# Spreading an expert's token weights over the partitions: two float32 passes from 32 rows, or one float32r matmul from 128 rows

## The chip, the cores and the metric

The kernel runs on one core of one Trainium2 chip. The metric is the device time of one execution in microseconds; the median of three runs is given, and one further execution was profiled.

## The reference, cut to what matters

The program is a chain of 18 stages on 256 tokens of 1024 features. Two of the stages (stage 1 and stage 4) are mixtures of experts; eight are feed-forward stages of a like shape. What an expert stage computes:

```python
g_w, g_idx = lax.top_k(softmax(xt @ w_group + b_group), 1)        # one of 4 groups
e_w, e_idx = lax.top_k(softmax(logits of that group), 2)          # two of its 8 experts
cw = einsum('tk,tke->te', g_w * e_w / sum(e_w), one_hot(expert))  # 256 tokens x 32 experts
hid = silu(einsum('td,edf->tef', xt, w_gate)) * einsum('td,edf->tef', xt, w_up)
y = einsum('tef,efd->td', hid * cw[:, :, None], w_down)
```

All 32 experts are computed for all tokens, and `cw` holds zeros for the experts that a token did not choose. A feed-forward stage is the same without `cw`, with 22 units of 128 hidden features.

## The kernel before

Activations lie feature by token: a tile of 128 partitions holds 128 features of 256 tokens. A product in float32 is made from three matmuls in float32r, a type in which TensorE takes one pass: weight and activation are each split into a high half (ScalarE copies to float32r) and a low half (VectorE or GpSimd subtracts the high half), and `mm3` (L591) adds high by high, high by low and low by high.

Weights stream through a ring of four slots (`ring`), one transfer of 1536 KB for one unit, issued in a fixed order by SyncE. From a slot a unit's three pieces (gate, up, down) are split into `wp`, which holds eight pieces; a piece's place is taken again once TensorE has used the old piece. In some of the units one more 1536 KB slot is read for work that belongs to later stages: ScalarE (`ada_act`) and VectorE (`ada_dve`) sum it into `ada_acc`, and one unit later TensorE (`ada_pe`) adds it up over the partitions with three float32 matmuls against `ones`. In an expert stage this starts in units 2, 4, ..., 30, and the three matmuls are issued in units 3, 5, ..., 31.

`glu_pe` sets the order on TensorE. For unit u it issues `products(u)` (48 float32r matmuls into one PSUM bank: gate in its left half, up in its right half), then what hooks and `ada_pe` there are, then `spread(u)`, then `down(u - 1)` (24 float32r matmuls that add into the stage's output in banks 0 to 3). `spread(u)` takes row u of `cwT`, a tile of 32 experts by 256 tokens, to all 128 partitions: the stationary operand is column u of the identity, broadcast over 128 columns, and both operands are float32 of 32 rows. The profile shows one float32 matmul call as two instructions.

The first two units have no `spread` and no `down` yet, for `cw` is not known. They come in unit 2 (`g.first` is 2), in the order `spread(0)`, `spread(1)`, `spread(2)`, `down(0)`, `down(1)`. Before them TensorE turns `cw` (L1598), and VectorE takes it out of PSUM and multiplies it with the token's scale into `cwT` (L1682).

`glu_dve` and `glu_act` hold the hidden part of a unit, which starts when `products(u)` is done: VectorE scales the gate (`rsb`), ScalarE takes Silu, VectorE multiplies with up, then with the spread weights, ScalarE makes the high half in `ex` and VectorE the low half. `down(u)` waits for the last of these. In each unit VectorE and ScalarE first split the next unit's pieces, then do the `ada` work where there is one, then the hidden part. In the last unit the pieces that are split first are those of the next stage. `spread(u)` waits for a free bank; in unit 2, `spread(1)` takes the bank of `products(0)` and `spread(2)` that of `products(1)`, each once VectorE has read the up half.

In the traces the matmuls carry the line of the helper `mm` (L271), so that they are told apart by their tiles: `pb<-hx,wp` is `products`, `pb<-ex,wp` is `down`, `pb<-ones,ada_acc` is `ada_pe`, and `pb<-sq,cst` is `spread`. `pb` is PSUM, `cwT` lies in `sq`, the identity in `cst`.

Of the kernel before, what the change touches and what calls it, by code (L numbers as in the profile page):

```python
# [11 lines left out]
FR = mybir.dt.float32r  # L12
I32 = mybir.dt.int32
ACT = mybir.ActivationFunctionType
AX = mybir.AxisListType

T = 256
# [307 lines left out]
def build_program(nc, stop=None):  # L325
# [6 lines left out]
    def sb(name, cols, dt=F32, rows=128):  # L332
        return ctx.enter_context(nc.sbuf_tensor(name, [rows, cols], dt))
# [34 lines left out]
    selw, selg = sb("selw", 128), sb("selg", 64)  # L368
    hr, bsum = sb("hr", 256, rows=48), sb("bsum", 256, rows=16)
    dl = sb("dl", 32)  # L370

    WK = 23 * 1024 - 64
    with nc.sbuf_tensor("wk", [128, WK], F32) as region:
# [45 lines left out]
    def row_spread(h, rows):  # L419
        a = ccol["ident"][0] + h  # L420
        return cst[0:rows, a:a + 1].to_broadcast([rows, 128])
# [25 lines left out]
    def bank(*key):  # L447
        return pb[where.get(key, 0)]
# [415 lines left out]
    def glu_pe(e, g, ready, hooks=(), cw=None):  # L864
        st = g.st
        bk.use([4, 5, 6, 7])

        def products(u):
            key = (st, "glu", u)
            ps = bk.take(e, key, (v_out, key))  # L870
            if u == 0:
                pair = g.pieces[u][0:2]
                for p in pair:
                    split_ready(e, p)
                for k in range(KD):
                    for sig, event in ready(k):
                        e.wait_ge(*sig[event])
                    for b, p in enumerate(pair):
                        ins = mm3(e, ps[:, b * T:(b + 1) * T], part((p.hi, p.lo), k * 128), in_hx(k), k == 0 == b,
                                  k == KD - 1)  # L880
                ins.then_inc(*product.up(("used", pair[0].at), ("used", pair[1].at), key))
                return
            for b, p in enumerate(g.pieces[u][0:2]):
                split_ready(e, p)
                for k in range(KD):
                    for sig, event in ready(k):
                        e.wait_ge(*sig[event])
                    ins = mm3(e, ps[:, b * T:(b + 1) * T], part((p.hi, p.lo), k * 128), in_hx(k), k == 0, k == KD - 1)
                ins.then_inc(*product.up(("used", p.at), *([key] if b else [])))

        def spread(u):
            key = (st, "cw", u)
            ps = bk.take(e, key, (v_out, key))
            e.wait_ge(*v_out[st, "cwT"])
            e.mm(ps[:, 0:T], row_spread(u, 32), cw, True, True).then_inc(*summed.up(key))

        def down(u):
            p = g.pieces[u][2]
            split_ready(e, p)
            e.wait_ge(*x_lo[st, "hid", u])  # L900
            for m in range(8):
                if u == 0 and m % 2 == 0:
                    y = bk.hold(e, m // 2, (st, "y", m // 2), (x_new, (st, m + 1)))
                y = pb[m // 2]
                ins = mm3(e, y[:, (m % 2) * T:(m % 2 + 1) * T], part((p.hi, p.lo), m * 128), (eh[u % 3], el[u % 3]),
                          u == 0 and m % 2 == 0, u == g.units - 1)
                if m % 2:
                    ins.then_inc(*product.up((st, "down", u, m), *([("used", p.at)] if m == 7 else [])))

        for u in range(g.units):  # L910
            products(u)
            if u < len(hooks):
                hooks[u]()
            if u in g.summed:
                ada_pe(e, g.summed[u])
            if u >= g.first:
                if cw is not None:
                    for n in range(0 if u == g.first else u, u + 1):
                        spread(n)
                for n in range(0, u) if u == g.first else [u - 1]:  # L920
                    down(n)
        down(g.units - 1)
        bk.use(range(8))
# [620 lines left out]
    def moe(st, l, slot0, after):  # L1544
# [32 lines left out]
        def pe(e):  # L1577
            def norm_and_logits():
                bk.hold(e, 0, (st, "var"), (v_step, (st, "var")))
                for k in range(KD):  # L1580
                    e.wait_ge(*g_step[st, "square", k])
                    ins = e.mm(bank(st, "var")[:, 0:T], ones[:, 0:128], Q3[:, k, :], k == 0, k == KD - 1)
                ins.then_inc(*summed.up((st, "var")))
                bk.hold(e, 1, (st, "lg"), (v_out, (st, "lg")))
                for k in range(KD):
                    ins = e.mm(bank(st, "lg")[0:36, 0:T], wr[:, k, :], H3[:, k, :], k == 0, k == KD - 1)
                ins.then_inc(*summed.up((st, "lg")))

            def logits_by_token():
                bk.hold(e, 2, (st, "lgt"), (v_out, (st, "lgt")))  # L1590
                e.wait_ge(*v_step[st, "lgT"])
                for b in range(2):
                    ins = e.tp(bank(st, "lgt")[:, b * 36:(b + 1) * 36], lgT[:, b * 128:(b + 1) * 128])
                ins.then_inc(*turned.up((st, "lgt")))

            def weights_by_expert():
                bk.hold(e, 3, (st, "cwt"), (v_out, (st, "cwT")))
                e.wait_ge(*v_step[st, "cw"])  # L1598
                for b in range(2):
                    ins = e.tp(bank(st, "cwt")[0:32, b * 128:(b + 1) * 128], cw[:, b, :])  # L1600
                ins.then_inc(*turned.up((st, "cwt")))

            glu_pe(e, G_, ready, (norm_and_logits, logits_by_token, weights_by_expert), cwT)

        def first_max(e, src, n, mx, eq, cum, oh, event):
            e.red(flat(mx), src, ALU.max).then_inc(*v_step.up())
# [48 lines left out]
        def dve(e):  # L1655
            for k in range(KD):
                e.ts(H3[:, k, :], X3[:, k, :], gain(k), None, ALU.mult).then_inc(*v_step.up((st, "h", k)))
                e.wait_ge(*v_step[st, "h", k])
                e.wait_ge(*x_hi[st, "h", k])
                e.tt(Hl[:, k, :], H3[:, k, :], Hh[:, k, :], ALU.subtract).then_inc(*x_lo.up((st, "h", k)))  # L1660

            def norm_and_logits():
                split_lo_v(e, G_.pieces[1])
                e.wait_ge(*summed[st, "var"])
                e.wait_ge(*v_step.last)
                e.ts(nv[:, :], bank(st, "var")[:, 0:T], 1.0 / D, 1e-6, ALU.mult, ALU.add).then_inc(*v_step.up((st, "var")))
                newton(e, rsb[:, :], nv[:, :], nm[:, :], nt[:, :], (st, "rs"))
                e.wait_ge(*v_step[st, "rs"])
                e.wait_ge(*summed[st, "lg"])
                e.tt(lgT, bank(st, "lg")[0:36, 0:T], rsb[0:36, :], ALU.mult).then_inc(*v_out.up((st, "lg")))  # L1670
                e.wait_ge(*v_out[st, "lg"])
                e.ts(lgT, lgT, pc(f"moe_b{l}", 0, 1, 36), None, ALU.add).then_inc(*v_step.up((st, "lgT")))

            def logits_by_token():
                e.wait_ge(*turned[st, "lgt"])
                e.copy(lg, bank(st, "lgt")[:, 0:72].rearrange("p (b n) -> p b n", b=2)).then_inc(*v_out.up((st, "lgt")))
                split_lo_v(e, G_.pieces[2])
                choose(e)

            def weights_by_expert():  # L1680
                e.wait_ge(*turned[st, "cwt"])
                e.tt(cwT, bank(st, "cwt")[0:32, 0:T], rsb[0:32, :], ALU.mult).then_inc(*v_out.up((st, "cwT")))  # L1682

            def finish(m, ps):
                e.tt(X3[:, m, :], X3[:, m, :], ps, ALU.add).then_inc(*x_new.up((st, m)))

            glu_dve(e, G_, finish, (norm_and_logits, logits_by_token, weights_by_expert), True)

        def act(e):
            for k in range(KD):  # L1690
                e.wait_ge(*x_new[st - 1, 7])
                e.act(Hh[:, k, :], X3[:, k, :], ACT.Copy, scale=gain(k)).then_inc(*x_hi.up((st, "h", k)))

            def norm_and_logits():
                split_hi(e, G_.pieces[1])

            def logits_by_token():
                split_hi(e, G_.pieces[2])
                for name, a in (("ge", ge), ("e2", e2)):
                    e.wait_ge(*v_step[st, name])  # L1700
                    e.act(a, a, ACT.Exp).then_inc(*a_step.up((st, name)))

            glu_act(e, G_, (norm_and_logits, logits_by_token, lambda: None), True)

        def pool(e):
            for k in range(KD):
# [1045 lines left out]
    def scalar_program(e):  # L2752
        e.wait_ge(s_in, 48)
        e.act(cact[:, :], pc("c", 0, 8), ACT.Silu).then_inc(*a_step.up("cact"))
        for s in stages:
            s.act(e)

# [64 lines left out]
```

## Time and profile before

| | |
|---|---|
| median of 3 runs | 4298.62 us (4298.27 to 4301.55) |
| the profiled execution: its time, its span | 4305.83 us, 4304.0 us |
| TensorE matmul busy | 3936.6 us, 91% of the span |
| VectorE, ScalarE, GpSimd busy | 2751.3, 1763.6, 1423.1 us |
| chain that ended last, TensorE's share | 78% |
| mean granted TensorE clock | 0.909 |
| spread matmuls in the trace | 128 instructions, 46.4 us busy |

The busy time of an engine is summed over stages with different limits, so what counts for this change is read in the stretch of an expert stage. A stretch of the first expert stage lies between 376 and 683 us of the span; the first `spread` instruction of the trace starts at 377.6 us and the last at 1215.7 us. A granted clock of 1.00 is 2.4 GHz, of 0.50 is 1.2 GHz.

### The profile page before, as it was taken

The numbers are of one execution on the slowest core, as the hardware profiler recorded it, in microseconds if no ns is written. First come the engines' busy times: TensorE is split into PE (matmuls) and PEld (weight loads), VectorE is DVE, ScalarE is ACT, GpSimd is POOL, SyncE is SP. The second block draws the span as 40 slices with busy tenths as digits, with TensorE's granted clock in tenths as the row PEclk, the third lists the DMA queues.
The fourth block names the chain that finished last, engine by engine and source line by source line (L and its number), as shares of the span: only waits on it lengthen the run. The fifth ranks groups of instructions, "written<-read, shape, count | busy, mean of one in ns | idle before, by whom it ended". The sixth has DMA issues, their size and how long they took to land.

```text
span 4304.0 us, 69799 instructions
## 1 busy us (share of the span) xinstructions
PE 3936.6 (91%) x29036; PEld 3571.0 (83%) x29036; DVE 2751.3 (64%) x5163; ACT 1763.6 (41%) x3006; POOL 1423.1 (33%) x794
## 2 busy tenths in 40 slices
PE   6998997989979898979999998989899999899899
PEld 6658997679979886769998967989869999767699
DVE  4446777467767766557776857767657743765543
ACT  3233444334444443234444634444444444432343
POOL 2003443034425432024453422435304444420143
PEclk9659998699989998979999988999969999879899
DMA  5104663146636530017575414757516644210143
GB/s 201 54 2 176 248 239 119 54 174 244 244 137 266 214 114 15 1 60 279 217 280 194 157 54 147 270 200 276 189 59 234 264 163 172 93 40 1 40 167 113
DMA packets 63691, 664.41 MB, mean 154 GB/s; under 512 B 7056, under 2 KB 7568, under 8 KB 7952
## 3 DMA queue, kind: packets, MB, share of 16 engines
q1 hardware_dynamic: 63376, 659.94, 40.8%
q8 instruction: 231, 3.78, 0.3%
q14 instruction: 84, 0.69, 0.0%
HBM read 658.86 MB, written 1.05 MB: 153 GB/s over the span
## 4 chain that ended last, share of the span: by engine, by line
PE 78%; DVE 15%; ACT 3%; issue 2%; POOL 0%; DMA 0%; SPq 0%; DVEq 0%; ACTq 0%
PE pb L271 76%; PE pb L278 3%; DVE wp L228 2%; DVE wk L240 2%; DVE wk L228 2%; ACT wp L266 2%; DVE sq L240 1%; DVE sq L228 1%; DVE ada_acc L240 1%; DVE hT L240 1%; ACT wk L266 1%; DVE nt L228 1%; DVE xT L240 1%; DVE hx L240 0%; DVE hx L228 0%
## 5 line engine op out<-in xcount | busy, mean ns | idle before, releaser
L271 PE MATMUL pb<-hx,wp 128*128 128x256 f32 x15744 | 1994.9, 287 | 75.7 <-DVE hx L228 38.3
L271 PEld LDWEIGHTS pb<-hx,wp 128*128 128x128 f32 x15744 | 1956.2, 196 | 94.7 <-issue 73.0
L228 POOL TENSOR_TENSOR wp<-ring,wp 128x512 fp32r<-128x512 f32 (+1 forms) x596 | 1255.4, 2124 | 2154.9 <-ACT wp L266 2154.9
L266 ACT ACTIVATE wp<-ring 128x1024 fp32r<-128x1024 f32 x936 | 940.9, 1046 | 276.0 <-PE pb L271 267.9
L228 DVE TENSOR_TENSOR wp<-ring,wp 128x1024 fp32r<-128x1024 f32 (+1 forms) x670 | 800.7, 1212 | 374.7 <-ACT wp L266 374.0
L271 PE MATMUL pb<-ex,wp 128*128 128x256 f32 x5856 | 760.5, 287 | 16.8 <-DVE ex L228 16.8
L271 PEld LDWEIGHTS pb<-ex,wp 128*128 128x128 f32 x5856 | 725.7, 194 | 38.6 <-issue 35.9
L240 DVE SCALAR_TENSOR_TENSOR ada_acc<-ring,cact,ada_acc 128x384 f32<-128x384 f32 x576 | 530.2, 984 | 58.1 <-ACT ada_acc L266 58.1
L271 PE MATMUL pb<-wk 128*128 128x128 f32 (+8 forms) x3136 | 494.8, 330 | 15.6 <-ACT wk L266 6.2
L271 PEld LDWEIGHTS pb<-wk 128*128 128x128 f32 (+4 forms) x3136 | 344.3, 193 | 161.3 <-issue 97.8
L228 DVE TENSOR_TENSOR sq<-sq,pb 128x256 f32<-128x256 f32 (+1 forms) x360 | 161.3, 448 | 319.4 <-ACT sq L266 272.0
L266 ACT ACTIVATE wk<-pb 128x256 f32<-128x256 f32 (+4 forms) x364 | 170.0, 475 | 446.7 <-PE pb L278 268.7
L266 ACT ACTIVATE sq<-pb 128x256 f32<-128x256 f32 (+1 forms) x216 | 87.8, 406 | 505.4 <-PE pb L271 429.6
L266 ACT ACTIVATE ex<-sq 128x256 fp32r<-128x256 f32 x240 | 100.3, 418 | 355.6 <-DVE sq L228 355.6
L266 ACT ACTIVATE wk<-wk 128x256 f32<-128x256 f32 (+4 forms) x301 | 127.7, 438 | 218.4 <-DVE wk L240 82.5
L228 DVE TENSOR_TENSOR ex<-sq,ex 128x256 fp32r<-128x256 f32 x240 | 132.4, 552 | 116.1 <-ACT ex L266 116.1
L228 POOL TENSOR_TENSOR wk<-wk,hT 128x256 f32<-128x256 f32 x32 | 22.6, 726 | 432.3 <-ACT wk L266 432.3
L278 PE MATMUL pb<-cst,wk 128*128 128x128 f32 (+1 forms) x612 | 129.8, 346 | 36.9 <-DVE wk L228 31.4
L266 ACT ACTIVATE sq<-sq 128x256 f32<-128x256 f32 (+1 forms) x68 | 27.5, 405 | 288.2 <-DVE sq L228 288.2
L278 PEld LDWEIGHTS pb<-cst,wk 128*128 128x128 f32 (+1 forms) x612 | 81.3, 168 | 69.9 <-DVE wk L228 30.6
L228 POOL TENSOR_TENSOR wk<-wk 128x256 f32<-128x256 f32 x88 | 72.3, 837 | 171.2 <-DVE wk L240 85.5
L228 DVE TENSOR_TENSOR wk<-pb,cst 128x256 f32<-128x256 f32 (+3 forms) x212 | 79.9, 426 | 66.8 <-PE pb L271 60.9
(175 smaller groups left out, 2840.6 us busy)
## 6 DMA issues: line engine op xcount, KB each, us to landing
ring<-weights SPq DMA_DIRECT2D x385, 1536.0 KB, 6.6
ring<-weights SPq DMA_DIRECT2D x41, 1024.0 KB, 4.8
ring<-weights SPq DMA_DIRECT2D x4, 512.0 KB, 10.1
cst<-consts SPq DMA_DIRECT2D x1, 2032.0 KB, 12.0
ring<-weights SPq DMA_DIRECT2D x1, 1280.0 KB, 5.4
prm<-params SPq DMA_DIRECT2D x1, 1258.0 KB, 7.6
ring<-weights SPq DMA_DIRECT2D x1, 1152.0 KB, 5.0
xT<-xT_in SPq DMA_DIRECT2D x1, 1024.0 KB, 4.9
```

Of the source, the lines that this page charges most:

```text
L228: return self.real.tensor_tensor(out, a, b, op) if self.real else Uncounted()
L240: return self.real.scalar_tensor_tensor(out=out, in0=a, scalar=s, in1=b, op0=op0, op1=op1)
L266: return self.real.activation(out, a, func, bias=bias, scale=scale, accum_out=accum)
L271: return self.real.matmul(out, l, r, start=start, stop=stop, skip_group_check=skip)
L278: return self.real.transpose(out, a, self.identity[base:base + n, base:base + n])
```

## The change

`spread(u)` becomes one float32r matmul of 128 rows. Two constant-sized tiles are new: `both_rows` (128 by 32), in which the identity of size 32 stands in rows 0 to 31 and again in rows 32 to 63, and `both_cw` (128 by 256), whose rows 0 to 31 are the high half of `cwT`, rows 32 to 63 its low half, and the rest zeros. Rows 64 to 127 of `both_rows` are columns 0 to 31 of the identity there, which are zeros. Summed over the rows, one matmul gives high plus low.

The low half is made where `cwT` is made: VectorE, behind `cwT`, waits for ScalarE's copy to float32r and subtracts. ScalarE's copy stands in its hook of unit 2, which was empty, ahead of the `ada` copies of that unit. The constant parts are written by four ScalarE instructions at the start of the program. `spread` waits for the low half in place of `cwT`.

```diff
+    both_rows, both_cw = sb("both_rows", 32, FR), sb("both_cw", 256, FR)
...
         def spread(u):
             key = (st, "cw", u)
             ps = bk.take(e, key, (v_out, key))
-            e.wait_ge(*v_out[st, "cwT"])
-            e.mm(ps[:, 0:T], row_spread(u, 32), cw, True, True).then_inc(*summed.up(key))
+            e.wait_ge(*x_lo[st, "cwT"])
+            e.mm(ps[:, 0:T], both_rows[:, u:u + 1].to_broadcast([128, 128]), cw, True, True).then_inc(*summed.up(key))
...
-            glu_pe(e, G_, ready, (norm_and_logits, logits_by_token, weights_by_expert), cwT)
+            glu_pe(e, G_, ready, (norm_and_logits, logits_by_token, weights_by_expert), both_cw[:, :])
...
             def weights_by_expert():
                 e.wait_ge(*turned[st, "cwt"])
                 e.tt(cwT, bank(st, "cwt")[0:32, 0:T], rsb[0:32, :], ALU.mult).then_inc(*v_out.up((st, "cwT")))
+                e.wait_ge(*x_hi[st, "cwT"])
+                e.tt(both_cw[32:64, :], cwT, both_cw[0:32, :], ALU.subtract).then_inc(*x_lo.up((st, "cwT")))
...
-            glu_act(e, G_, (norm_and_logits, logits_by_token, lambda: None), True)
+            def weights_by_expert():
+                e.wait_ge(*v_out[st, "cwT"])
+                e.act(both_cw[0:32, :], cwT, ACT.Copy).then_inc(*x_hi.up((st, "cwT")))
+
+            glu_act(e, G_, (norm_and_logits, logits_by_token, weights_by_expert), True)
...
         e.act(cact[:, :], pc("c", 0, 8), ACT.Silu).then_inc(*a_step.up("cact"))
+        for a in (0, 32):
+            e.act(both_rows[a:a + 32, :], ident[a:a + 32, a:a + 32], ACT.Copy).then_inc(*a_step.up("rows"))
+        e.act(both_rows[64:128, :], ident[64:128, 0:32], ACT.Copy).then_inc(*a_step.up("rows"))
+        e.act(both_cw[64:128, :], C("half")[64:128, 0:256], ACT.Copy, scale=0.0).then_inc(*a_step.up("rows"))
```

## Rows read from the trace of the kernel before

**Rows 1.** The page's head, and the chain that ended last by engine.
```profile
span 4304.0 us, 69799 instructions
...
PE 78%; DVE 15%; ACT 3%; issue 2%; POOL 0%; DMA 0%; SPq 0%; DVEq 0%; ACTq 0%
```

**Rows 2.** Groups by shape, TensorE: count, busy us, mean ns, idle before.
```profile
L271 PE MATMUL pb<-sq,cst 32*128 32x256 f32 x128 | 46.4, 443 | 12.4 <-DVE sq L228 12.4
```

**Rows 3.** Timeline, TensorE, expert stage: start us, us, engine, line, tiles, count.
```profile
442.60 5.92 PE L271 MATMUL pb<-hx,wp 128*128 128x256 f32 x48
448.45 0.69 PE L271 MATMUL pb<-sq,cst 32*128 32x256 f32 x2
...
452.04 5.92 PE L271 MATMUL pb<-hx,wp 128*128 128x256 f32 x48
457.80 0.73 PE L271 MATMUL pb<-ones,ada_acc 128*128 128x1 f32 x6
458.46 0.69 PE L271 MATMUL pb<-sq,cst 32*128 32x256 f32 x2
...
462.06 5.92 PE L271 MATMUL pb<-hx,wp 128*128 128x256 f32 x48
```

**Rows 4.** The same view in a feed-forward stage.
```profile
2208.96 5.92 PE L271 MATMUL pb<-hx,wp 128*128 128x256 f32 x48
...
2217.60 5.92 PE L271 MATMUL pb<-hx,wp 128*128 128x256 f32 x48
2223.36 0.73 PE L271 MATMUL pb<-ones,ada_acc 128*128 128x1 f32 x6
...
2226.91 5.92 PE L271 MATMUL pb<-hx,wp 128*128 128x256 f32 x48
```

**Rows 5.** Timeline, weight loads around one spread in the expert stage.
```profile
487.37 0.29 PEld L271 LDWEIGHTS pb<-sq,cst 32*128 32x128 f32 x2
487.99 0.53 PEld L271 LDWEIGHTS pb<-ex,wp 128*128 128x128 f32 x4 [0.33 <-issue]
```

**Rows 6.** By tile: weight loads, ns min/median/max, first and last start.
```profile
L271 PEld LDWEIGHTS pb<-sq,wk x320: 190/192/192, 1669.9 to 4030.0; 128*128 128x128 f32 x160
...
L271 PEld LDWEIGHTS pb<-sq,cst x128: 180/183/328, 377.6 to 1215.5; 32*128 32x128 f32 x128
```

**Rows 7.** Windows: us, busy of PE, PEld, DVE, ACT, POOL, clock, DMA, GB/s.
```profile
450.00:500.00 50.00, 50.00 (x399) 48.03 (x398) 36.57 (x54) 22.32 (x32) 21.51 (x10) 1.00 0.66 252
...
2218.00:2256.00 38.00, 38.00 (x320) 38.00 (x319) 26.49 (x35) 18.67 (x27) 17.38 (x8) 1.00 0.70 273
```

**Rows 8.** Timeline, VectorE and ScalarE, where the first weights are made.
```profile
377.08 0.41 DVE L228 TENSOR_TENSOR sq<-pb,rsb 32x256 f32<-32x256 f32 x1 [0.49 <-PE pb L278]
377.42 3.24 DVE L240 SCALAR_TENSOR_TENSOR ada_acc<-ring,cact,ada_acc 128x384 f32<-128x384 f32 x6
...
374.64 1.11 ACT L266 ACTIVATE ada_acc<-ring,cact 128x384 f32<-128x384 f32 x2
375.77 1.28 ACT L266 ACT_TABLE_LOAD   x1
381.62 0.42 ACT L266 ACTIVATE sq<-sq 128x256 f32<-128x256 f32 x1 [4.57 <-DVE sq L228]
```

**Rows 9.** Timeline, TensorE, the third spread and the first down.
```profile
385.15 1.22 PE L271 MATMUL pb<-sq,cst 32*128 32x256 f32 x2 [1.38 <-DVE sq L228]
386.29 7.53 PE L271 MATMUL pb<-ex,wp 128*128 128x256 f32 x48
```

**Rows 10.** Windows, the stretch in which TensorE starts again.
```profile
380.00:390.00 10.00, 6.07 (x22) 4.70 (x23) 6.45 (x16) 3.44 (x7) 0.00 (x0) 0.51 0.43 157
```

**Rows 11.** The chain in order of time, first expert stage: start us, us, what.
```profile
385.15 271.73 PE pb L271 x2132
656.92 0.94 issue
...
669.72 5.91 DVE wp L228 x2
```

**Rows 12.** Timeline, TensorE, the last two downs of the stage.
```profile
673.19 3.14 PE L271 MATMUL pb<-ex,wp 128*128 128x256 f32 x24
678.37 4.24 PE L271 MATMUL pb<-ex,wp 128*128 128x256 f32 x24 [2.04 <-DVE ex L228]
```

**Rows 13.** Timeline, ScalarE, start of the program.
```profile
13.63 0.21 ACT L266 ACTIVATE cact<-prm 128x8 f32<-128x8 f32 x1 [11.64 <-DMA cst<-consts]
17.40 2.95 ACT L266 ACTIVATE wp<-ring 128x1024 fp32r<-128x1024 f32 x3 [3.56 <-DMA ring<-weights]
```

## The prediction

> **What bounds the kernel now.** I read the chain that ended last first: TensorE holds 78% of it [rows 1], so an edit of TensorE's work can reach the end. The groups by shape then give what is edited: 128 instructions, two for each of 64 spreads, 46.4 us busy [rows 2]. That is not yet what a spread costs, since the neighbours' stalls are not in it. For that I laid out TensorE's order in one pair of units of the expert stage [rows 3] and in one pair of a feed-forward stage [rows 4], which has the same 48 and 24 matmuls in each unit and no spread. The windows show that TensorE has no idle time in either stretch and that the clock is granted in full, 1.00, which is 2.4 GHz [rows 7]. The chain in order of time says the same of the first expert stage: it is TensorE's alone for 271.73 us from 385.15 us, until 656.88 us, and then leaves it [rows 11]. So whatever a unit of this stretch loses on TensorE, the kernel loses.
>
> **What a spread costs now.** A unit without `ada_pe` takes 452.04 - 442.60 = 9.44 us in the expert stage [rows 3] and 2217.60 - 2208.96 = 8.64 us in the feed-forward stage [rows 4]: the spread costs 0.80 us. A unit with `ada_pe` takes 462.06 - 452.04 = 10.02 us and 2226.91 - 2217.60 = 9.31 us: there it costs 0.71 us. The two instructions are 0.69 us of it; the rest lies around them, for the weight loads stood idle for 0.33 us before those of `down` [rows 5].
>
> **What the new one costs.** It has the shape of its neighbours: 128 rows, 128 columns, 256 moving, float32r. 72 of those take 8.64 us [rows 4], so one takes 0.12 us. No row shows a float32r matmul whose stationary operand is one column broadcast. From below I take 0.12 us as well, since nothing of 256 columns in the rows costs less. From above, 0.80 us: the old pair is the nearest row with a broadcast operand. I take 0.12 us, for two reasons. The broadcast load is itself no slower, 183 ns against 192 ns for a plain one [rows 6]. And a change of type costs nothing: six float32 instructions of 128 rows between float32r ones add 9.31 - 8.64 = 0.67 us to the feed-forward unit [rows 4], 0.11 us each with both changes. What is left to explain the stall at the spread is the 32 rows and the length of the float32 passes, and both go.
>
> The weight loads of a 32-row operand take about as long as those of 128 rows [rows 6]. The Trainium skill says so too, on the page "TensorE: Matmul & The Clock Gate", section "Part 2: What happens when you issue a matmul", under LDWEIGHTS: row count does not matter, the 128 columns do. By that rule filling the rows buys nothing, and only one instruction in place of two is left; the stall at the spread would stay. The trace agrees on the duration of the load, and does not show whether the load could have started earlier with full rows; rival B below is this case, and its time is worked out from rows.
>
> **The steady part.** The spreads of units 3 to 29 lie in the stretch that is TensorE's. 14 of these units have `ada_pe` (3, 5, ..., 29) and 13 have none (4, ..., 28). Saved: 14 x (0.71 - 0.12) + 13 x (0.80 - 0.12) = 8.26 + 8.84 = 17.1 us in a stage, 34.2 us in both.
>
> The work that feeds this stretch must keep up with 2 x 0.12 + 8.64 + 9.31 = 18.19 us for a pair in place of 19.46 us. VectorE is busy for 36.57 of 50 us, so 14.2 us in a pair, which would be 78%. Reading rises from 252 GB/s to about 270 GB/s; the feed-forward stretch already moves 273 GB/s with no idle TensorE [rows 7]. I charge nothing.
>
> **The end of a stage.** The spreads of units 30 and 31 are saved for nothing. At 656.92 us the chain goes to the splits and the `ada` work of unit 30, then to the next stage's splits on VectorE (5.91 us from 669.72 us) [rows 11], then to the hidden part of unit 31, and TensorE waits 2.04 us for it before the last `down` [rows 12]. None of that starts sooner when spreads 30 and 31 are shorter, so the wait grows to about 2.04 + 0.68 + 0.59 = 3.3 us. The longer gap can make the clock fall sooner. The last `down` takes 4.24 us against 3.14 us for the one before it [rows 12], so it runs partly at the low clock already; wholly at 1.2 GHz it would be 24 x 0.24 = 5.8 us. The added cost is between 0 and 1.5 us a stage; I take 0.5, 1.0 in both.
>
> **The start of a stage.** The new wait sits on VectorE behind `cwT`. Behind it are queued the six `ada` steps (3.24 us) and then the hidden part of units 0, 1 and 2, for which TensorE waits [rows 8, 9]. ScalarE used to make its two `ada` copies (1.11 us) during the choice of experts; now they stand behind its copy of `cwT`. A ScalarE copy of 256 columns takes 0.42 us, one `ada` copy 0.56 us, and only the first is needed for VectorE's next step: 0.42 + 0.56 + about 0.06 for two hand-overs is 1.04 us late. The subtraction (0.41 us, as `cwT` itself) runs beside that `ada` copy, so it adds nothing; without that cover it would add 0.41. The table load of 1.28 us now comes last and would end at 377.49 + 0.45 + 1.11 + 1.28 = 380.3 us; the first Silu of this part is due at 381.62 + 1.04 us, so it stays hidden.
>
> Given back here: `spread(2)` is directly on the path. It and its stall take 386.29 - 385.15 = 1.14 us [rows 9] at the low clock (0.51 granted over this stretch [rows 10]), and one float32r matmul at half the rate takes 0.24 us. Net 1.04 - 0.90 = 0.14, say 0.2 us a stage, 0.4 in both. If the low clock lasts shorter or longer because of it, this is worth up to 2 us either way.
>
> **The start of the program.** Four ScalarE copies (0.2 to 0.42 us each, under 1.7 us) go between 13.84 us and 17.40 us, where ScalarE waits for the first weights for 3.56 us [rows 13]. Nothing, unless the weights land at once: then up to 1.7 us.
>
> **The sum.** -34.2 + 1.0 + 0.4 = -32.8 us. On the profiled span, 4304.0 us, it gives 4271.2 us. That execution took 4305.83 us, 7.2 us above the median of the runs, so its like would take 4273.0 us, and the median 4298.62 - 32.8 = 4265.8, say 4266 us.
>
> **Rivals.**
> A is the forecast.
>
> B: the load of the spread, or that of the `down` behind it, still cannot start under the matmul ahead, because the stall comes from the broadcast operand. Then the spread is one instruction in place of two but keeps its gaps: half of 0.80, 0.40 us. Saved: 13 x 0.40 + 14 x 0.31 = 9.5 us a stage, 19.1 in both, less 1.4: 4281 us. For it: the idle 0.33 us of [rows 5] is no part of either instruction. Against: the load of a broadcast column is as quick as others.
>
> C: nothing is lost at the ends: the two last spreads count too (2 x 1.27 = 2.5 us more) and the clock charge of 1.0 falls away: 4262 us. Against it stands the wait of 2.04 us [rows 12].
>
> D: the feed becomes the bound. VectorE, ScalarE or the ring cannot follow below 19.46 us a pair, and TensorE waits out what it saved: about 4300 us, no change. Against it is the feed-forward pair of 17.95 us [rows 4], which has two VectorE steps less in each unit.
>
> E, on the other side: the new wait at the start of a stage. If ScalarE's copy is late, VectorE is held with all the work behind it and TensorE stands idle longer, and after a longer idle time the granted clock stays low for longer. It must cost over 17.1 us a stage to make the kernel slower; 1.04 us of delay is shown by rows, and the low stretch now costs at most half of some 10 us [rows 10]. With twice that stretch and two such delays it would be near 7 us a stage. To decide it would take three or four times this; its time from there is 4308 us and up.
>
> **How the numbers follow.** A 0.70, B 0.12, C 0.10, D 0.05, E 0.03. A's own range is 4262 to 4272 us. 8 times in 10 I expect 4259 to 4275 us, which holds A and C; B is left out below its full price, D and E wholly. Faster by over 0.2% (8.6 us, about what a measurement of this kernel can tell from no change) is A, B and C: 0.92. Within it is D: 0.05. Slower is E: 0.03.
>
> **What the profile after will show.** The spread as one instruction of 128 rows, and a pair of units 18.2 us apart (8.76 and 9.43); a pair of 18.7 us or more says B, one with idle TensorE D. The wait before the last `down` near 3.3 us; if still near 2.0, C. The first `ada` step some 1.0 us behind `cwT`, and the start of `down(0)` about 9.3 us behind `cwT`, as before. Wrong would be the forecast if a float32r matmul with a broadcast stationary operand has a price of its own, since no row shows one.

## The result

| | before | after |
|---|---|---|
| median, us | 4298.99 (4298.27 to 4301.55, 4 runs) | 4263.18 (4261.05 to 4266.42, 4 runs) |
| ratio, 95% interval | | 0.9916 (0.9899 to 0.9933) |
| the profiled execution: time, span, us | 4305.83, 4304.0 | 4266.42, 4264.6 |

The changed kernel is 35.8 us faster; 32.8 us were forecast, and 4263.18 us lies in the range of 4259 to 4275 us.

TensorE in an expert stage after the change, in order of time (start us, us, engine, line, tiles, count); these rows answer to [rows 3]:

```profile
401.16 5.92 PE L271 MATMUL pb<-hx,wp 128*128 128x256 f32 x48
406.92 0.28 PE L271 MATMUL pb<-both_cw,both_rows 128*128 128x256 f32 x1
407.03 3.04 PE L271 MATMUL pb<-ex,wp 128*128 128x256 f32 x24
409.90 5.92 PE L271 MATMUL pb<-hx,wp 128*128 128x256 f32 x48
415.67 0.73 PE L271 MATMUL pb<-ones,ada_acc 128*128 128x1 f32 x6
416.25 0.36 PE L271 MATMUL pb<-both_cw,both_rows 128*128 128x256 f32 x1
...
419.33 5.92 PE L271 MATMUL pb<-hx,wp 128*128 128x256 f32 x48
```

A unit without `ada_pe` takes 409.90 - 401.16 = 8.74 us and one with it 419.33 - 409.90 = 9.43 us. Against the feed-forward stage, 8.64 and 9.31 us [rows 4], the new spread costs 0.10 and 0.12 us, where the old one cost 0.80 and 0.71 us.

The weight loads around one new spread, and the same loads by tile (ns min/median/max, first and last start), answer to [rows 5] and [rows 6]:

```profile
443.15 0.19 PEld L271 LDWEIGHTS pb<-both_cw,both_rows 128*128 128x128 f32 x1
443.26 0.90 PEld L271 LDWEIGHTS pb<-ex,wp 128*128 128x128 f32 x7
...
L271 PEld LDWEIGHTS pb<-both_cw,both_rows x64: 185/192/288, 376.5 to 1177.9; 128*128 128x128 f32 x64
```

The load of `down` starts 0.11 us behind that of the spread, with no idle time ahead of it, and both matmuls start 0.11 us behind their loads (443.26 and 443.38 us). A broadcast column of 128 rows loads in 192 ns, as the plain operand of 128 rows in [rows 6].

The windows of this stretch (us, busy of PE, PEld, DVE, ACT, POOL, clock, DMA share, GB/s) answer to [rows 7]:

```profile
420.00:450.00 30.00, 30.00 (x253) 30.00 (x253) 23.68 (x34) 13.29 (x20) 13.14 (x6) 1.00 0.71 279
```

TensorE has no idle time, VectorE is busy for 79% (78% were worked out) and 279 GB/s are moved. The feed followed.

The start of the stage, VectorE, ScalarE and TensorE in order of time ([rows 8], [rows 9] before):

```profile
375.08 0.41 DVE L228 TENSOR_TENSOR sq<-pb,rsb 32x256 f32<-32x256 f32 x1 [0.49 <-PE pb L278]
375.97 0.41 DVE L228 TENSOR_TENSOR both_cw<-sq,both_cw 32x256 fp32r<-32x256 f32 x1 [0.48 <-ACT both_cw L266]
376.48 3.26 DVE L240 SCALAR_TENSOR_TENSOR ada_acc<-ring,cact,ada_acc 128x384 f32<-128x384 f32 x6
...
375.52 0.41 ACT L266 ACTIVATE both_cw<-sq 32x256 fp32r<-32x256 f32 x1 [2.79 <-DVE sq L228]
375.85 1.10 ACT L266 ACTIVATE ada_acc<-ring,cact 128x384 f32<-128x384 f32 x2
376.97 1.28 ACT L266 ACT_TABLE_LOAD   x1
...
384.23 0.58 PE L271 MATMUL pb<-both_cw,both_rows 128*128 128x256 f32 x1 [2.02 <-DVE sq L228]
384.61 7.29 PE L271 MATMUL pb<-ex,wp 128*128 128x256 f32 x48
```

The first `ada` step starts 376.48 - 375.08 = 1.40 us behind the start of `cwT`; before it was 377.42 - 377.08 = 0.34 us [rows 8]. It comes 1.06 us later (1.04 were worked out). `down(0)` starts 9.53 us behind the start of `cwT`, 9.21 us before.

The end of the stage, the chain in order of time and TensorE ([rows 11], [rows 12] before):

```profile
384.23 253.36 PE pb L271 x2104
637.64 0.94 issue
...
650.43 5.95 DVE wp L228 x2
...
652.71 3.03 PE L271 MATMUL pb<-ex,wp 128*128 128x256 f32 x24
659.12 3.11 PE L271 MATMUL pb<-ex,wp 128*128 128x256 f32 x24 [3.38 <-DVE ex L228]
```

TensorE's part of the chain is 253.36 us in place of 271.73 us and ends at the same unit (28 instructions fewer, one for each of the spreads 2 to 29); the wait before the last `down` has grown from 2.04 to 3.38 us. What was not expected stands in the last row: the last `down` takes 3.11 us, not 4.24 us.

What TensorE does next takes back most of this. The first of these lines is from the kernel before, the second from the changed one:

```profile
685.22 1.02 PE L271 MATMUL pb<-ones,sq 128*128 128x1 f32 x8 [2.61 <-DVE sq L228]
```

```profile
664.84 1.84 PE L271 MATMUL pb<-ones,sq 128*128 128x1 f32 x8 [2.61 <-DVE sq L228]
```

Behind the shorter `down` the same eight matmuls take 0.82 us more; from the end of `down` to the next stage's `products` 0.67 is granted before and 0.59 after. From the start of the last `down` to the start of those `products` it is 692.56 - 678.37 = 14.19 us before and 672.99 - 659.12 = 13.87 us after, so 0.3 us are left of the 1.1 us. The second expert stage shows the same: the wait grows from 2.05 to 3.38 us, the last `down` takes 3.11 us in place of 4.34 us, and 14.30 us become 13.87 us.

At the start of the program the four copies fit in ahead of the first weights (start us, us), as [rows 13] let expect:

```profile
13.56 0.71 ACT L266 ACTIVATE both_rows<-cst 32x32 fp32r<-32x32 f32 x3
14.18 0.40 ACT L266 ACTIVATE both_cw<-cst 64x256 fp32r<-64x256 f32 x1
17.20 2.95 ACT L266 ACTIVATE wp<-ring 128x1024 fp32r<-128x1024 f32 x3 [2.62 <-DMA ring<-weights]
```

### The profile page after: what moved, and what is told of

It reads as the page before. It is cut to its first block, busy times and chain, and to the rows that moved or that the text cites. A ratio compares the mean times of both kernels' runs of the same rounds, so it can differ in the third digit from the quotient of the medians.

```text
span 4264.6 us, 69679 instructions
## 1 busy us (share of the span) xinstructions
PE 3890.2 (91%) x28972; PEld 3556.0 (83%) x28972; DVE 2749.3 (64%) x5165; ACT 1766.3 (41%) x3012; POOL 1420.4 (33%) x794
## 4 chain that ended last, share of the span: by engine, by line
PE 78%; DVE 16%; ACT 3%; issue 2%; POOL 0%; DMA 0%; SPq 0%; DVEq 0%; ACTq 0%
PE pb L271 75%; PE pb L278 3%; DVE wp L228 2%; DVE wk L240 2%; DVE wk L228 2%; ACT wp L266 2%; DVE sq L228 1%; DVE sq L240 1%; DVE ada_acc L240 1%; DVE hT L240 1%; ACT wk L266 1%; DVE nt L228 1%; DVE xT L240 1%; DVE hx L240 0%; DVE hx L228 0%
## 5 line engine op out<-in xcount | busy, mean ns | idle before, releaser
L271 PE MATMUL pb<-ex,wp 128*128 128x256 f32 x5856 | 751.8, 285 | 19.5 <-DVE ex L228 19.5
```

The source lines that it names most:

```text
L271: return self.real.matmul(out, l, r, start=start, stop=stop, skip_group_check=skip)
```

## The experiments

Ratios are against the kernel before, run on the same chip. Its medians in the three groups of runs were 4301.07 us (e1 to e4), 4300.51 us (e5 to e8) and 4299.68 us (e9, e10). Except e1, all start from the changed kernel. Each reading of the profile is from one profiled execution.

**e1: two float32 passes, with 128 rows.** The edit of the kernel before (`both_cw` is in float32, with zeros from row 32 on; there is no copy and no subtraction of halves):

```diff
             e.wait_ge(*v_out[st, "cwT"])
-            e.mm(ps[:, 0:T], row_spread(u, 32), cw, True, True).then_inc(*summed.up(key))
+            e.mm(ps[:, 0:T], ident[:, u:u + 1].to_broadcast([128, 128]), cw, True, True).then_inc(*summed.up(key))
...
-                e.tt(cwT, bank(st, "cwt")[0:32, 0:T], rsb[0:32, :], ALU.mult).then_inc(*v_out.up((st, "cwT")))
+                e.tt(both_cw[0:32, :], bank(st, "cwt")[0:32, 0:T], rsb[0:32, :], ALU.mult).then_inc(*v_out.up((st, "cwT")))
```

> The spread as two float32 instructions again, but with 128 rows (identity column and token weights followed by zeros), without the copy and subtraction of the changed kernel. Theory R (rows): the idle time around the old spread comes from operands of 32 rows; the price falls from 0.80/0.71 us in a unit to two plain float32 instructions of 256 columns, 0.45 to 0.5 us, a pair of units takes 18.85 to 18.95 us, and the time is about 4299 - 2 x (13 x 0.32 + 14 x 0.23) = 4284 us. Theory P (passes): rows do not matter, the stall belongs to the slow float32 passes; pair 19.46 us, time 4299 us.

Measured: 4285.51 us, ratio 0.9960 (0.9945 to 0.9975). TensorE in order of time (the tile name `both_cw,cst` is this spread):

```profile
420.27 5.92 PE L271 MATMUL pb<-hx,wp 128*128 128x256 f32 x48
426.03 0.59 PE L271 MATMUL pb<-both_cw,cst 128*128 128x256 f32 x2
...
429.32 5.92 PE L271 MATMUL pb<-hx,wp 128*128 128x256 f32 x48
...
439.06 1.12 PE L271 MATMUL pb<-hx,wp 128*128 128x256 f32 x8
```

Units of 9.05 and 9.74 us, so 0.41 and 0.43 us a spread. Theory R: filling the rows alone takes 0.39 and 0.28 us off, with both passes kept. Theory P is out, and the time is 1.5 us above the 4284 us expected.

**e2 and e3: one float32r pass, with 32 and with 64 rows.**

```diff
-            e.mm(ps[:, 0:T], both_rows[:, u:u + 1].to_broadcast([128, 128]), cw, True, True).then_inc(*summed.up(key))
+            e.mm(ps[:, 0:T], both_rows[0:32, u:u + 1].to_broadcast([32, 128]), cw[0:32, :], True, True).then_inc(*summed.up(key))   # e2
+            e.mm(ps[:, 0:T], both_rows[0:64, u:u + 1].to_broadcast([64, 128]), cw[0:64, :], True, True).then_inc(*summed.up(key))   # e3
```

> The changed kernel with the spread matmul over rows 0 to 31 alone (the high half; the low half of the token weights is left out of the sum). Theory R: one pass, but the weight load cannot run ahead; 0.3 to 0.45 us a spread, pair 18.6 to 18.8 us, time 4273 to 4280 us. Theory P: 0.12 us a spread, pair 18.17 us, time 4263 us.

> The changed kernel with the spread matmul over rows 0 to 63 (both halves, without the rows of zeros). Theory R: as with 32 rows, for 64 rows are not the full array either: 0.3 to 0.45 us a spread, pair 18.6 to 18.8 us, time 4273 to 4280 us. Theory P: 0.12 us, pair 18.17 us, 4263 us; then the rows of zeros are needless.

Measured: 4283.64 us, ratio 0.9959 (0.9945 to 0.9973), and 4287.53 us, 0.9966 (0.9953 to 0.9979). TensorE with 32 rows, and behind it the weight loads around one spread:

```profile
420.85 5.92 PE L271 MATMUL pb<-hx,wp 128*128 128x256 f32 x48
426.70 0.38 PE L271 MATMUL pb<-both_cw,both_rows 32*128 32x256 f32 x1
...
429.98 5.92 PE L271 MATMUL pb<-hx,wp 128*128 128x256 f32 x48
...
439.66 0.52 PE L271 MATMUL pb<-hx,wp 128*128 128x256 f32 x3
...
426.70 0.18 PEld L271 LDWEIGHTS pb<-both_cw,both_rows 32*128 32x128 f32 x1
427.00 2.93 PEld L271 LDWEIGHTS pb<-ex,wp 128*128 128x128 f32 x24
```

and with 64 rows:

```profile
415.31 5.92 PE L271 MATMUL pb<-hx,wp 128*128 128x256 f32 x48
421.16 0.38 PE L271 MATMUL pb<-both_cw,both_rows 64*128 64x256 f32 x1
...
424.45 5.92 PE L271 MATMUL pb<-hx,wp 128*128 128x256 f32 x48
...
434.14 5.92 PE L271 MATMUL pb<-hx,wp 128*128 128x256 f32 x48
```

32 rows: 9.13 and 9.68 us a unit, 0.49 and 0.37 us a spread. 64 rows: 9.14 and 9.69 us, so 0.50 and 0.38 us. Theory P is out. Theory R has the kind right and the size too low: 0.49 and 0.50 us lie above its 0.3 to 0.45 us, and both times above its 4273 to 4280 us. The rows of zeros are not needless: 64 rows hold all that is computed, and cost as much as 32.

The loads show where the time goes. With 32 rows the load of the spread starts at the same instant as its matmul (426.70 us), and that of `down` with the first matmul of `down` (427.00 and 427.01 us). With 128 rows both loads start 0.11 us ahead, under the matmul before them. The overlap is missing on the way into the spread and on the way out.

**e8: four float32r matmuls of 32 rows.** As e2, each issued four times.

```diff
+            for _ in range(3):
+                e.mm(ps[:, 0:T], both_rows[0:32, u:u + 1].to_broadcast([32, 128]), cw[0:32, :], True, True)
             e.mm(ps[:, 0:T], both_rows[0:32, u:u + 1].to_broadcast([32, 128]), cw[0:32, :], True, True).then_inc(*summed.up(key))
```

> As e2_f32r_32rows (high half alone, low half left out), with four such matmuls in place of one, each writing the same bank. Unit without ada_pe now 8.64 + 0.49 us. Theory S (a stall where the number of rows changes, once into and once out of it): each further matmul costs 0.11 to 0.12 us, unit 9.13 + 0.35 = 9.48 us. Theory L (every matmul of 32 rows waits for its load): each costs as much as the first, at least 0.3 us, unit 10.0 us or more.

Measured in a single run: 4309.45 us. TensorE:

```profile
425.38 5.92 PE L271 MATMUL pb<-hx,wp 128*128 128x256 f32 x48
431.23 0.73 PE L271 MATMUL pb<-both_cw,both_rows 32*128 32x256 f32 x4
...
434.85 5.92 PE L271 MATMUL pb<-hx,wp 128*128 128x256 f32 x48
```

The unit takes 9.47 us, 0.34 us more than with one: 0.11 us for each further matmul. So Theory S: not each matmul of few rows is slow, the change of row count is, once for the whole group. Row counts other than 32, 64 and 128 were not run.

**e4 and e9: the old spread in some units.** In e4 units 30 and 31 alone have the old spread, in e9 units 3 to 29 alone.

```diff
+            if u >= 30:                 # e4;  e9: if 3 <= u < 30
+                e.mm(ps[:, 0:T], row_spread(u, 32), sq[0:32, 1792:2048], True, True).then_inc(*summed.up(key))   # cwT
+                return
```

> The changed kernel with the old spread (float32, 32 rows) in units 30 and 31 alone. Theory T (the last two spreads are hidden behind the wait of the last down): the wait before the last down is 2.0 to 2.1 us instead of 3.38, its start stays the same distance behind cwT (284.0 us in stage 1), and the time is 4263 us, the same. Rival C: both are paid, 2 x 1.27 = 2.5 us more, 4265.7 us. If the shorter idle time keeps the clock up, the last down takes 3.1 us, if the length of the idle time has nothing to do with it, it may take 3.1 or 4.3.

> The changed kernel with the old spread in units 3 to 29 alone, the new one in units 0, 1, 2, 30 and 31. Theory T (the whole gain lies in units 3 to 29): pair 19.46 us, the last down starts 301.5 to 302 us behind the transposes instead of 284.5 us, time 4263 + 34.2 = 4297 us, within 0.2% of the kernel before. Rival: a part of the gain lies in the other units, the time is below 4290 us.

Measured: e4 4259.95 us, ratio 0.9904 (0.9889 to 0.9919); e9 4304.6 us, ratio 1.0014 (1.0002 to 1.0025). The last two `down`s of e4, with the wait between them, and the last of e9:

```profile
647.17 3.14 PE L271 MATMUL pb<-ex,wp 128*128 128x256 f32 x24
652.35 3.11 PE L271 MATMUL pb<-ex,wp 128*128 128x256 f32 x24 [2.04 <-DVE ex L228]
```

```profile
376.46 0.40 PE L278 MATMUL pb<-cst,sq 128*32 128x128 f32 x2 [0.91 <-DVE sq L228]
...
678.28 4.32 PE L271 MATMUL pb<-ex,wp 128*128 128x256 f32 x24 [3.36 <-DVE ex L228]
```

The profiles are as Theory T has them. Spreads 30 and 31 at the old price shorten the wait to 2.04 us and cost nothing. With the old price in units 3 to 29 the last `down` starts 678.28 - 376.46 = 301.8 us behind the transposes, as in the kernel before (301.72 us), and the gain is gone. The time of e9 is 7.6 us above the 4297 us expected, and its ratio lies just above 1; the cause of these few microseconds is open.

The two kernels also settle a side question. The last `down` takes 3.11 us behind a wait of 2.04 us (e4) and of 3.38 us (changed), and 4.24 us behind 2.04 us (before) and 4.32 us behind 3.36 us (e9). The second expert stage repeats it (3.10, 3.11, 4.34 and 4.43 us), and in e8 it takes 3.11 us in the first stage and 4.61 us in the second, both times behind a wait of 2.00 us. The length of the wait does not decide it.

**e5 and e6: the changed kernel again, and with the copy and the subtraction later at the start of a stage.** In e6 ScalarE makes its `ada` copies ahead of the copy of `cwT`, and VectorE subtracts behind its `ada` steps:

```diff
-            if u < len(hooks):
+            if u < len(hooks) and u != g.first:
                 hooks[u]()
...
             if g.ada.get(u) is not None:
                 ada_act(e, g.ada[u], st)
+            if u < len(hooks) and u == g.first:
+                hooks[u]()
...
             if g.ada.get(u) is not None:
                 ada_dve(e, g.ada[u])
+            if cw and u == g.first:
+                e.wait_ge(*x_hi[st, "cwT"])
+                e.tt(both_cw[32:64, :], sq[0:32, 1792:2048], both_cw[0:32, :], ALU.subtract).then_inc(*x_lo.up((st, "cwT")))
...
-                e.wait_ge(*x_hi[st, "cwT"])
-                e.tt(both_cw[32:64, :], cwT, both_cw[0:32, :], ALU.subtract).then_inc(*x_lo.up((st, "cwT")))
```

> The changed kernel once more, as the measure for the two beside it. 4263 us, ratio 0.9916; it says how far two measurements of one kernel lie apart on another chip.

> The changed kernel with the new wait taken off the path: in unit 2 ScalarE makes its two ada copies before it waits for cwT, as in the kernel before, and VectorE subtracts behind the six ada steps. Theory W (the new wait costs 0.99 us of the start of each expert stage): the first ada step follows cwT at once, down(0) starts 9.0 us behind the transposes instead of 9.96 us, the whole kernel is 2.0 us faster than the changed one, 4261 us. Rival: ScalarE's copy is late on another engine's account, and down(0) stays at 9.9 us.

Measured: e5 4266.05 us, ratio 0.9921 (0.9907 to 0.9934); e6 4267.59 us, ratio 0.9921 (0.9908 to 0.9935). In e5 the last `down` takes 3.11 and 3.10 us in the two stages. For e6 4261 us were expected, and no gain shows. Its TensorE, at the start and at the end of the stage:

```profile
376.88 0.40 PE L278 MATMUL pb<-cst,sq 128*32 128x128 f32 x2 [0.91 <-DVE sq L228]
...
386.33 7.51 PE L271 MATMUL pb<-ex,wp 128*128 128x256 f32 x48
...
661.05 5.46 PE L271 MATMUL pb<-ex,wp 128*128 128x256 f32 x24 [3.37 <-DVE ex L228]
```

`down(0)` starts 9.45 us behind the transposes in place of 9.96 us. Half of the 1.06 us comes back, for the subtraction (0.42 us) now lies bare on VectorE's path; the expectation had left it out. At the end the last `down` takes 5.46 us in place of 3.11 us, in both stages. From its start to the `products` of the next stage it is 676.60 - 661.05 = 15.55 us in place of 13.87 us, so this execution loses 1.7 us a stage there and gained 0.5 us at the start. It was the second slowest of five (4272.07 us of 4259.48 to 4272.64 us), and no profile shows whether the last `down` took as long in the fastest. The windows of it in the three kernels, before, changed and e6:

```profile
678.40:682.60 4.20, 4.20 (x24) 3.92 (x24) 2.24 (x6) 2.23 (x6) 0.00 (x0) 0.68 0.09 39
```

```profile
659.12:662.20 3.08, 3.08 (x24) 2.90 (x24) 2.09 (x6) 1.63 (x5) 0.00 (x0) 1.00 0.12 51
```

```profile
661.05:666.51 5.46, 5.46 (x24) 5.17 (x24) 2.26 (x6) 2.24 (x6) 0.00 (x0) 0.50 0.07 27
```

Granted are 0.68, 1.00 and 0.50: TensorE is at 1.2 GHz for a part, for nothing and for all of it.

**e7 and e10: the next stage's second split behind the last hidden part.** e7 has e6's start, e10 the changed kernel's.

```diff
             elif u + 1 == g.units:
-                split_lo_v(e, early(st + 1))
+                split_lo_v(e, early(st + 1)[:2] if cw else early(st + 1))
...
+            if cw and u + 1 == g.units:
+                split_lo_v(e, early(st + 1)[2:])
```

> As e6_lead, and in the last unit of an expert stage VectorE splits only the first of its two early pieces of the next stage before the hidden part, the second behind it. Theory T (the last down waits for VectorE's splits, not for TensorE): the wait of 3.38 us before the last down falls to below 0.6 us; the second split then holds back the sums into xT, so that 1.0 to 2.6 us a stage are left, 4256 to 4259 us. If the wait stays at 3.38 us, what holds the last down is something else.

> The changed kernel with the split order of e7 (the second early split behind the hidden part of the last unit) and without the reordered start of e6. From e7: the wait before the last down is 0.0 us instead of 3.38 us, and 3 to 3.5 us a stage of it reach the next stage, if the clock does not take them back: 4256 to 4260 us. If the last down runs at the low clock again (5 us instead of 3.1 us), the kernel is no faster than the changed one.

Measured: e7 4261.08 us, ratio 0.9909 (0.9896 to 0.9923); e10 4258.63 us (4257.44 to 4260.12), ratio 0.9904 (0.9888 to 0.9921). The end of the stage in e10:

```profile
653.22 6.18 PE L271 MATMUL pb<-ex,wp 128*128 128x256 f32 x48
662.02 1.84 PE L271 MATMUL pb<-ones,sq 128*128 128x1 f32 x8 [2.61 <-DVE sq L228]
```

The two last `down`s run without a gap, 48 matmuls in 6.18 us, and so they do in e7 (6.17 us). So what held the last one was VectorE's splits. e7 misses its 4256 to 4259 us, e10 lies in its 4256 to 4260 us. e10 has the lowest median here: all its runs lie below all runs of the changed kernel (4261.05 us and up). The two intervals overlap, so its lead over the changed kernel, 4.6 us against the first median and 7.4 us against e5's, is likely and small. Its profile has it too: from the transposes to the next stage's `products` 670.17 - 375.11 = 295.06 us in the first expert stage, in place of 672.99 - 374.65 = 298.34 us.

## Why the prediction was right

**What a spread costs.** 0.80 and 0.71 us was the right loss, read from the two kinds of stage, and 0.12 us the right price of the new one (0.10 and 0.12 us). In units without `ada_pe` the runs divide it: the old pair 0.80 us, full rows only (e1) 0.41 us, one pass only (e2) 0.49 us, both 0.10 us. Rows are worth 0.39 us, the second pass 0.31 us, and they add up to the 0.70 us saved. With `ada_pe` they are worth 0.28 and 0.34 us, together 0.62 us of 0.59 us. The prediction could not tell these two apart, and did not need to. It misplaced one row: the 0.33 us for which the weight loads stood idle [rows 5] end at 487.99 us and the two old instructions run from 487.37 to 488.06 us, so that this idle time lies within their 0.69 us and not around it. Rival B, that the broadcast operand makes the stall, is out: e1 and the changed kernel have it and no such stall. By the Trainium skill ("TensorE: Matmul & The Clock Gate", "Part 2: What happens when you issue a matmul", LDWEIGHTS) the row count does not matter for how long a load takes. The loads' durations agree, 183 ns with 32 rows and 192 ns with 128 [rows 6]. What the rows cost lies elsewhere, in when the load can start: the prediction left that open, and e1, e2 and e3 show it to be worth 0.39 us.

**The steady part and the feed.** 17.1 us a stage was forecast for the steady part, 16.9 us with the 0.2 us of the start taken off. The last `down` starts 659.12 - 374.65 = 284.47 us behind the transposes, and 678.37 - 376.65 = 301.72 us before: 17.25 us less, with the start in it. In the second expert stage it is 284.61 us in place of 301.63 us, 17.02 us less. The feed held at 18.17 us a pair, so rival D is out.

**The ends.** Spreads 30 and 31 were saved for nothing, as said (e4), which puts rival C's first half out. Its second half, that the charge for the clock falls away, came true, and its 4262 us lie nearer to the 4263.18 us than the forecast does; the wait of 3.38 us and e4 decide between the two, not the time. The charge for the clock had the wrong sign. The step was "the longer gap can make the clock fall sooner": +0.5 us a stage were taken, and the last `down` became 4.24 - 3.11 = 1.1 us shorter. e4, e8 and e9 show that the wait is not what matters. This gain was luck: nothing in the prediction foresaw it, and in e6, which differs from the changed kernel only at the start of a stage, the same `down` took 5.46 us. The small matmuls behind it took 0.8 us of it back, so that the ends cost 0.3 and 0.4 us less than before instead of 0.5 us more. The bound from below was drawn at no change, though the 4.24 us already held 1.1 us of low clock that could go; the range should have reached below zero. By their rows the two stages save 17.25 + 0.32 + 17.02 + 0.43 = 35.0 us up to the next `products`, 2.2 us more than the forecast. The ends are 1.75 us of this (0.75 us gained and 1.0 us charged), the steady part and the start the rest.

**The start.** The new wait cost 1.06 us (1.04 forecast), and the shorter `spread(2)` gave back less than thought: it took 384.61 - 384.23 = 0.38 us, not 0.24 us. `down(0)` came 0.3 us later, and 0.2 were taken. Rival E, which needed 17.1 us, was far off.

**The span.** It is 39.4 us shorter, the median 35.8 us. 35.0 us of this are those of the two stages. 2.0 us lie ahead of `cwT` of the first expert stage, which starts at 375.08 us in one profile and at 377.08 us in the other; up to there only the four copies at the start are new. In e5, the same changed kernel on another chip, the transposes start at 370.92 us in place of 374.65 us, so profiles of one kernel differ by more than this, and no cause within the change is sought for it. The part between the two stages is as long as before (227.0 us), and the long part behind the second is 2.3 us shorter, for which no cause was sought either.

**Open.** What decides whether and at which instant of a stage the clock falls was not settled. The runs show its effect and rule out the length of the wait before the last `down`.

## What to carry to other kernels

Price a small matmul by the difference between two like stretches, with it and without it: its busy time gave 0.69 us here, its loss was 0.80 us. Where one matmul of 32 or 64 rows stands in a stream of matmuls of 128 rows, padding it with zeros up to 128 is worth trying (0.10 us in place of 0.49 or 0.50 us here), with the low half in the room; 64 rows gained nothing over 32. A saving counts only up to the unit where the chain leaves TensorE, and what an edit gains at the start of a stage (0.5 us in e6) can be outweighed by where the clock falls at its end (1.7 us in the profiled execution). Follow such a stretch to the next fixed point: `down` alone seems to gain 1.1 us, of which 0.3 us reach the next stage.

## What the runs showed of the hardware that was not expected

- A matmul of 32 or 64 rows among those of 128 costs 0.49 or 0.50 us instead of 0.10 us. Four in a row cost only 0.34 us more than one (e8), so it is paid for the group, at the change of row count. The weight loads show it on both sides: that of the spread and that of the next `down` start with their own matmuls, not ahead of them as with 128 rows.
- Behind the float32 matmuls of `ada_pe` the same change costs less, 0.37 us against 0.49 us with 32 rows.
- The same 24 matmuls at the end of a stage took 3.11, 4.24, 4.32 and 5.46 us in kernels that differ elsewhere, at granted clocks of 1.00, 0.68, 0.66 and 0.50. The figure comes back in the second expert stage within 0.11 us in these four, but not in e8 (3.11 and 4.61 us). What the shorter `down` gains over the kernel before, the eight small matmuls behind it lose in large part: 1.84 us in place of 1.02 us.
